# A hybrid attention layer: the opening of its attention, its up weights and gate stores moved, and latent attention's rotary scores in two row tiles of 64 rows

## The reference

```
h = rms_norm(x, g_in)
a_q, a_k, a_v, a_gate, b_cq, b_ckv, b_kr, b_gate, m_q, m_gate = split(h @ w_in)
out_a = swa_sink_attention(...) * silu(a_gate)      # 16 heads of 64, chunks of 64, window 128
qb  = rms_norm(b_cq) @ w_q_up                       # 4 heads of 128 + 64
kvb = rms_norm(b_ckv) @ w_kv_up                     # 4 heads of 128 + 128
qb_nope = rms_norm(qb[..., :128]);  qb_rope = rope(rms_norm(qb[..., 128:]))
kb_nope = rms_norm(kvb[..., :128]); vb = kvb[..., 128:]
kb_rope = rope(rms_norm(b_kr))                      # one key of 64 for all heads
scores  = (qb_nope @ kb_nope + qb_rope @ kb_rope) * 192 ** -0.5    # chunk-causal
out_b = softmax(scores) @ vb * silu(b_gate)
out_m = memory_cross_attention(...) * silu(m_gate)  # 4 heads of 128 over 256 memory tokens
return x + concat(out_a, out_b, out_m) @ w_o
```

## Time and profile before

| | us |
|---|---|
| median of 3 runs | 1538.54 (1537.95 to 1540.06) |
| the profiled execution | 1540.13 |
| its span, first to last instruction | 1538.3 |
| TensorE busy | 1490.5 |
| VectorE, ScalarE, GpSimd busy | 588.8, 442.9, 107.7 |

### The profile page before, as it was taken

The page is one execution under the profiler, slowest core; times in us unless marked ns, Lnnn a source line. Parts: engine busy times, 40 slices in busy tenths (PEclk is TensorE's granted clock), DMA queues, the critical chain, the costliest instruction groups (busy, mean ns, idle before and its releaser), DMA issues.

```text
span 1538.3 us, 17896 instructions
## 1 busy us (share of the span) xinstructions
PE 1490.5 (97%) x7192; PEld 1217.7 (79%) x7192; DVE 588.8 (38%) x829; ACT 442.9 (29%) x799; POOL 107.7 (7%) x82
## 2 busy tenths in 40 slices
PE   7999999999999999999998997889998999999998
PEld 6888888888888888887886786656788888888886
DVE  6633241442523221312227576875456321020202
ACT  6430311303030111112124455973356311010110
POOL 0201000202000000000101122000000000000000
PEclk9999999999999999999999997999999999999999
DMA  8121231131223121211426422440022214141301
GB/s 324 49 56 55 96 109 55 41 109 41 69 81 109 43 108 50 100 55 55 154 106 217 149 73 65 130 122 14 28 90 90 98 53 158 47 163 41 109 27 55
DMA packets 42101, 138.29 MB, mean 90 GB/s; under 512 B 4160, under 2 KB 8256, under 8 KB 41792
## 3 DMA queue, kind: packets, MB, share of 16 engines
q1 hardware_dynamic: 28384, 84.42, 16.4%
q0 software_dynamic: 13520, 53.12, 9.9%
q10 hardware_dynamic: 144, 0.02, 0.0%
HBM read 109.23 MB, written 28.32 MB: 89 GB/s over the span
## 4 chain that ended last, share of the span: by engine, by line
PE 91%; ACT 5%; DVE 2%; issue 1%; DMA 1%; POOL 0%; ACTq 0%; SPq 0%; DVEq 0%
PE ps L1352 26%; PE ps L1353 26%; PE ps L1354 26%; ACT a_p L752 3%; PE ps L1562 2%; PE ps L1525 2%; PE ps L1526 2%; PE ps L1543 1%; PE ps L1568 1%; PE ps L1529 1%; DMA w_raw<-in_w 1%; PE ps L1400 0%; PE ps L1399 0%; DVE w_lo L861 0%; PE ps L1547 0%
## 5 line engine op out<-in xcount | busy, mean ns | idle before, releaser
L1352 PE MATMUL ps<-w_hi,h_hi 128*128 128x512 f32 x1152 | 449.9, 391 | 10.1 <-DVE h_lo L872 9.4
L1353 PE MATMUL ps<-w_lo,h_hi 128*128 128x512 f32 x1152 | 449.6, 390 | 0.0
L1354 PE MATMUL ps<-w_hi,h_lo 128*128 128x512 f32 x1152 | 449.6, 390 | 0.0
L861 DVE TENSOR_TENSOR w_lo<-w_raw,w_hi 128x1024 fp32r<-128x1024 f32 x120 | 149.9, 1249 | 743.1 <-ACT w_hi L576 742.9
L576 ACT ACTIVATE w_hi<-w_raw 128x1024 fp32r<-128x1024 f32 x122 | 129.1, 1058 | 894.6 <-PE ps L1354 880.0
L1352 PEld LDWEIGHTS ps<-w_hi,h_hi 128*128 128x128 f32 x1152 | 217.0, 188 | 55.1 <-issue 9.3
L1354 PEld LDWEIGHTS ps<-w_hi,h_lo 128*128 128x128 f32 x1152 | 216.9, 188 | 45.3
L1353 PEld LDWEIGHTS ps<-w_lo,h_hi 128*128 128x128 f32 x1152 | 217.0, 188 | 44.9
L1353 PE MATMUL ps<-h_lo,w_hi 128*128 128x512 f32 x512 | 199.4, 389 | 0.0
L1354 PE MATMUL ps<-h_hi,w_lo 128*128 128x512 f32 x512 | 199.4, 389 | 0.0
L1352 PE MATMUL ps<-h_hi,w_hi 128*128 128x512 f32 x512 | 199.4, 389 | 0.0
(11 more groups left out here) (234 smaller groups left out, 1446.5 us busy)
## 6 DMA issues: line engine op xcount, KB each, us to landing
w_raw<-in_w SPq DMA_DIRECT2D x122, 512.0 KB, 3.3
gate_s<-T POOLq DMA_DIRECT2D x4, 2048.0 KB, 7.0
mixed<-gate_s POOLq DMA_DIRECT2D x16, 512.0 KB, 4.7
x_raw<-in_xT SPq DMA_DIRECT2D x7, 1024.0 KB, 18.2
aq_s<-T POOLq DMA_DIRECT2D x2, 2048.0 KB, 7.5
a_q_at<-aq_s SPq DMA_DIRECT2D x16, 256.0 KB, 3.7
S<-in_x POOLq DMA_DIRECT2D x2, 2048.0 KB, 9.7
T<-in_x POOLq DMA_DIRECT2D x2, 2048.0 KB, 12.0
```

Source lines behind the costliest of these rows:

```text
L861: v.tensor_tensor(w_lo[:, n % SPLIT, :], w_raw[:, n % RAW, :], w_hi[:, n % SPLIT, :].bitcast(F32), ALU.subtract).then_inc(lo_ready, 1)
L1352: mm(out, a_hi, b_hi, start=start, stop=False)
L1353: mm(out, a_hi, b_lo, start=False, stop=False)
L1354: return mm(out, a_lo, b_hi, start=False, stop=stop)
```

## The change

- Gates: `gate_part_out` releases each of its four parts (`gate_done`), and POOL stores each as it is ready (`last_stored`), where it stored all four at the end.
- Up weights: they are loaded during the last gate group, not in the memory stage. Their high parts are made by ScalarE in four pieces behind the chunks 5, 6, 7 and 8 of the memory stage, and the low parts by VectorE in four pieces, ahead of the low parts of the chunks 10, 11, 14 and 15.
- Opening: the window keys' transposes come ahead of the last `up`, the memory keys' inside it; then query 0, `up_back(5)`, score 0, query 1, `up_back(6)`, score 1, query 2, `up_back(7)`. ScalarE and VectorE have an order to match. The load of `vM` stands behind query loads 4 and 5, and the gate loads no longer wait for the last `up_norm`.
- Latent attention: `qrT` holds every head in both halves of the partitions (ScalarE copies each head into its half, two DMAs copy the other half), `krT` holds the keys in both, without zeros. A step's keys are cut into two halves of w = (t+1)*64, one per PSUM bank; each half has a nope matmul over 128 rows, and the two rotary matmuls use rows 0 to 63 and rows 64 to 127. VectorE's maximum and ScalarE's exponent read two banks.

```diff
+        q_rope = qrT[:].rearrange("p (a o) s -> p a o s", o=2)
@@ sync: queries' loads
+                if isinstance(i, int) and i == 0:
+                    sp.wait_ge(u_done, TT)
+                    sp.dma_start(vM[:], vm_s.rearrange("(t p) n -> p t n", p=P)).then_inc(vm_loaded, 16)
+                if isinstance(i, int) and i == 0:
+                    sp.wait_ge(u_qr_kept, 2 * TT)
+                    for o in range(2):
+                        sp.dma_start(q_rope[64 - 64 * o:128 - 64 * o, :, o, :], q_rope[64 * o:64 * o + 64, :, o, :]
+                                     ).then_inc(qr_copied, 16)
@@ gpsimd
+                    pool.wait_ge(w_used, first(G_LAST) + 5)
+                    pool.dma_start(uq_raw[:], io["w_q_up"].rearrange("k p n -> p k n")).then_inc(uq_loaded, 16)
+                    pool.wait_ge(w_used, first(G_LAST) + 7)
+                    pool.dma_start(ukv_raw[:], io["w_kv_up"].rearrange("k p n -> p k n")).then_inc(ukv_loaded, 16)
...
+                else:
+                    for q in range(4):
+                        pool.wait_ge(gate_done, q + 1)
+                        pool.dma_start(dst[:, q, :], src[:, q, :]).then_inc(last_stored, 16)
...
-            pool.wait_ge(u_done, TT)
@@ scalar
             for c in range(1, CPG):
                 high(CH_MEM + c)
+                if c >= 5:
+                    up_high(c - 5)
...
+            high(n)
+            up_high(3)
...
-                    for g in range(2):
-                        rows = slice(64 * g, 64 * g + 64)
-                        a.activation(krT[rows, g, :], ps[rows, 3:5, :].rearrange("p a n -> p (a n)"), ACT.Copy).then_inc(kr_kept, 1)
-                    act.wait_ge(uq_loaded, 32)
-                    a.activation(uq_hi[:], uq_raw[:], ACT.Copy).then_inc(up_hi, 1)
+                    a.activation(krT[:], ps[:, 3:5, :].rearrange("p a n -> p (a n)"), ACT.Copy).then_inc(kr_kept, 1)
...
             def up_keep(t):
                 act.wait_ge(u_qr, t + 1)
-                a.activation(qrT[:, :, t * P:(t + 1) * P],
-                             ps[:, 2 if t < TT - 1 else 1, 0:256].rearrange("p (h s) -> p h s", h=2), ACT.Copy
-                             ).then_inc(u_qr_kept, 1)
+                for o in range(2):
+                    rows = slice(64 * o, 64 * o + 64)
+                    a.activation(q_rope[rows, :, o, t * P:(t + 1) * P],
+                                 ps[rows, rotary_place(t)[0], rotary_place(t)[1]].rearrange("p (h s) -> p h s", h=2), ACT.Copy
+                                 ).then_inc(u_qr_kept, 1)
...
+            keys_kept()
+            up_out(TT - 1, between=memory_keys_kept)
+            up_square(TT - 1)
+            turn_q(A, 0, 0)
+            up_keep(TT - 3)
+            turn_q(A, 1, 1)
+            bring_in(ACT.Exp)
+            up_keep(TT - 2)
             exponents(A, 0, 0)
             turn_q(A, 2, 0)
+            up_keep(TT - 1)
@@ vector
-            for g in range(2):
-                rows = slice(64 - 64 * g, 128 - 64 * g)
-                v.memset(krT[rows, g, :], 0.0).then_inc(zeroed, 1)
...
+            up_low(0)
             low(n + 2)
+            up_low(1)
             low(n + 3)
...
+                do(v.memset(sc[0:CHUNK, 1, w - CHUNK:w], -BIG))
+                do(v.tensor_reduce(st[:, par, 0, 0:1], sc, XY, ALU.max))
...
+            up_keep(TT - 3)
+            up_squares(TT - 1)
+            maximum(A, 0, 0, first=True)
+            up_keep(TT - 2)
+            up_norm(TT - 1)
+            maximum(A, 1, 1)
+            up_keep(TT - 1)
@@ tensor: score of latent attention
-                        mm(out, qnT[:, h, q], knT[:, h, a:b], start=True, stop=False)
-                        ins = mm(out, qrT[:, h // 2, q], krT[:, h % 2, a:b], start=False, stop=True)
+                    for o in range(2):
+                        mm(ps[:, bank + o, 0:w], qnT[:, h, q], knT[:, h, o * w:(o + 1) * w], start=True, stop=False)
+                    for o in range(2):
+                        rows = slice(64 * o, 64 * o + 64)
+                        ins = mm(ps[:, bank + o, 0:w], qrT[rows, h, q], krT[rows, o * w:(o + 1) * w],
+                                 start=False, stop=True)
@@ tensor: opening
+            window_keys()
+            up(TT - 1, between=memory_keys)
+            pe.wait_ge(km_kept, 1)
+            queries_ready(A, 0, 0, 0)
+            turn_q(A, 0)
+            up_back(TT - 3)
...
+            scores_ready(A, 0)
+            score(A, 0, 0)
+            queries_ready(A, 1, 1, 0)
+            turn_q(A, 1)
+            up_back(TT - 2)
+            scores_ready(A, 1)
+            score(A, 1, 1)
+            queries_ready(A, 2, 0, 1)
+            turn_q(A, 0)
+            up_back(TT - 1)
             pe.wait_ge(u_qn_kept, TT)
             pe.wait_ge(u_kn_kept, TT)
```

More of the change, by code:

```diff
@@ L28 @@
 X = mybir.AxisListType.X
+XY = mybir.AxisListType.XY
 P = 128
@@ L177, in layer @@
         vB = at("vB", [P, TT, BH * BV], F32, R0 + 32768)
-        qrT = at("qrT", [P, BH // 2, SEQ], F32, R0 + 49152)
-        krT = at("krT", [P, 2, SEQ], F32, R0 + 57344)
+        qrT = at("qrT", [P, BH, SEQ], F32, R0 + 49152)
+        q_rope = qrT[:].rearrange("p (a o) s -> p a o s", o=2)
         ident = small("ident", [P, P])
@@ L645, in _, with up_high @@
                         memory_square(c - 6)
+            def up_high(part):
+                if part < 2:
+                    act.wait_ge(uq_loaded, 16)
+                    hi, raw = uq_hi[:, 2 * part:2 * part + 2, :], uq_raw[:, 2 * part:2 * part + 2, :]
+                else:
+                    act.wait_ge(ukv_loaded, 16)
+                    hi, raw = ukv_hi[:, part - 2, :], ukv_raw[:, part - 2, :]
+                a.activation(hi, raw, ACT.Copy).then_inc(up_hi, 1)
             def gate_sigmoid_part(q):
@@ L706, in up_out @@
                              ).then_inc(u_q_out, 1)
+                if between:
+                    between()
                 act.wait_ge(u_up, t + 1)
@@ L1074, in _, with up_low @@
                 assert len(todo) <= 2 * (CPG - 1)
+            def up_low(part):
+                dve.wait_ge(up_hi, part + 1)
+                if part < 2:
+                    lo, raw, hi = (u[:, 2 * part:2 * part + 2, :] for u in (uq_lo, uq_raw, uq_hi))
+                else:
+                    lo, raw, hi = (u[:, part - 2, :] for u in (ukv_lo, ukv_raw, ukv_hi))
+                v.tensor_tensor(lo, raw, hi.bitcast(F32), ALU.subtract).then_inc(up_lo, 1)
             def gate_part_out(q):
@@ L1133, in _ @@
             low(n + 5)
+            up_low(2)
             low(n + 6)
-            dve.wait_ge(up_hi, 1)
-            v.tensor_tensor(uq_lo[:], uq_raw[:], uq_hi[:].bitcast(F32), ALU.subtract).then_inc(up_lo, 1)
+            up_low(3)
             low(n + 7)
             up_in(0)
-            dve.wait_ge(up_hi, 2)
-            v.tensor_tensor(ukv_lo[:], ukv_raw[:], ukv_hi[:].bitcast(F32), ALU.subtract).then_inc(up_lo, 1)
             dve.wait_ge(mem_free, 4)
-            dve.wait_ge(t_stored, 16 * (NTOK + 1))
+            dve.wait_ge(last_stored, 64)
+            dve.wait_ge(t_stored, 16 * NTOK)
             v.tensor_copy(T[:, 0:2, :], S[:, 0:2, :]).then_inc(t_ready, 1)
@@ L1275, in m_normal @@
                                        .to_broadcast([P, MH, NMEM]), ALU.mult)
-            for step in range(TT + 3):
-                if 0 <= step - 1 < TT:
+            for step in range(TT):
+                if step >= 1:
                     up_squares(step - 1)
-                if step == TT + 2:
-                    maximum(A, 0, 0, first=True)
-                    maximum(A, 1, 1)
                 if step >= 3:
@@ L1572, in begin @@
             def begin(at_, last, n_last, k):
+                if at_ is B and k == 1:
+                    pe.wait_ge(qr_copied, 32)
                 if k >= 1:
@@ L1604, in tiles_of, with window_keys, memory_keys @@
                 return body
-            for step in range(TT + 3):
-                if 1 <= step < TT:
+            def window_keys():
+                pe.wait_ge(kn_loaded, 16)
+                pe.wait_ge(u_clo, TT)
+                for t in range(TT):
+                    ins = turn(ps[:, t // 4, t % 4 * P:(t % 4 + 1) * P], a_kn[:, t, :], ident[:])
+                ins.then_inc(kn_turned, 1)
+            def memory_keys():
+                pe.wait_ge(km_loaded, 16)
+                pe.wait_ge(kn_kept, 1)
+                for h in range(MH):
+                    for t in range(2):
+                        k = 2 * h + t
+                        ins = turn(ps[:, k // 4, k % 4 * P:(k % 4 + 1) * P], c_km[:, t, h * P:(h + 1) * P], ident[:])
+                ins.then_inc(km_turned, 1)
```

136 lines of the change are left out of this document (46 added, 90 removed).

## The result

| | us, median | runs |
|---|---|---|
| before | 1538.54 | 1537.95 to 1540.06 |
| after | 1530.52 | 1528.77 to 1531.45 |
| ratio | 0.9943, 95% interval 0.9931 to 0.9954 | |

One execution of the changed kernel took 4261 us; the median is that of all five (1530.10 without it), the range and the ratio are over the other four. The change gains 8.0 us where the forecast had 20.2, and the time lies above the range of 1511 to 1527. A second set of runs of the same kernel gave 1529.89 beside 1538.96 for before (0.9934, interval 0.9920 to 0.9947).

The account below looks back on a forecast made before the run. TensorE, busy 97% of the span, was taken as the bound, with four places where it waits or runs slowly. Terms -8.3 + 1.0 - 8.0 - 4.9 = -20.2 us gave 1518.3 us as median, range 1511 to 1527.

Parts of the forecast that it names:

- part 3: Opening of windowed attention (929 to 965): reordered, chunk 2's exponents start 26.7 us behind the last up projection, not 35.3; -8.0 us.
- Part 1: Last gates' stores in four parts, up weights earlier (811 to 871): first up projection at 862.3, not 870.56; -8.3 us.
- Part 2: Up loop (871 to 936): a second copy of the rotary queries makes four steps pay 0.25 us; +1.0 us.
- Rival (a): TensorE's clock falls to 1.2 GHz again in the new opening: 3.5 us in all, 1521.8 us; chance 0.20.
- Part 4: Latent attention (1028 to 1132): rotary matmuls run side by side in two row tiles, 1.2 us per head; -4.9 us.
- (c): Latent attention: the row tiles' instructions pair only in part, 6.4 us more, 1524.7 us; chance 0.04.
- (d): Latent attention: nothing pairs, +9.8 us instead of -4.9, 1533 us; chance 0.05.
- (e): Latent attention: the drain and weight loads at tiling changes are hidden, 1510.4 us; chance 0.05.
- (b): The weight load at 833 is late anyway, so its 6.5 us stay, 1525 us; chance 0.09.
- (f): The opening's half clock lasts through windowed attention: 35 us, 1553 us; chance 0.05, shared with other losses.

Follow-up runs that it names:

- Experiments 2 and 3: The changed kernel with the qrT copies halved and issued later, 1521.60 us; and with only the vM load moved behind windowed attention's last load, 1527.28 us.
- 7: The changed kernel with its two qrT copies issued by ScalarE behind its first copy of a_pT, another queue than the query loads: 1528.95 us.
- the twin: The changed kernel with latent attention's row tiles undone: zero-padded krT, a single copy of the rotary queries, no copies of qrT: 1528.05 us.
- Experiment 11: The late copies kernel with each up projection's 12 matmuls into bank 3 first, waiting for the rotary query copies only before bank 2: 1518.88 us.
- late copies: The changed kernel with the qrT copies split by head pair, issued behind chunk 13's query load and windowed attention's last load: 1521.60 us.
- experiment 9: The late copies kernel with both rotary matmuls of a step on rows 0 to 63, sharing one row tile: 1536.14 us.

## Why the prediction was wrong

**The step that failed** stands at the end of part 3: "The chains through POOL [...] and SP (vM and the copies of `qrT` behind query loads 4 and 5) have 4 us or more of slack here." I asked when the copies are needed, 50 us later, and not what they take from the loads beside them. In the trace the copies, with vM beside them, cost 8.64 us, all of it in one stall of 8.0 us and a stretch at half clock behind it. Nor was the slack 4 us: query load 6 is issued at 954.63 and wanted at 959.4, and of these 4.8 us such a load alone takes 3.7. Experiments 2 and 3 show that the copies cause it and vM lengthens it; 7 shows that it is no matter of SP's queue. The warning stood in the working, the size did not. Steady windowed attention moves 137 GB/s at a DMA share of 0.48, which makes 285 when full (an estimate). From 949.85 to 954.63 the order issues 2.7 MB, query load 6 included: vM, the two copies, a gate load, two query loads and a value load. At 285 GB/s that takes 9.4 us, until 959.3: no slack left, but no stall of 8 us. At the 378 GB/s of the full stretch at 833 it takes 7.1. The rest is that the full engines moved only 203 to 227 GB/s here, and that is known only from after.

**Part 1, -8.3.** Measured -7.44, and 0.27 of the difference comes from stages ahead of 811. No load of 9 us (the longest of 822 to 851 is 7.1), no half clock at 845: right. The weight load at 833 took 5.3 us, not 3.4 to 4, and landed at 838.7, where the prediction has it wanted at 838.8. The memsets, put at nothing, are worth something in the new order: with them back, in the twin, TensorE idles 2.08 us at 843.58.

**Part 2, +1.0.** Measured +1.91. The mechanism was right and the size off. The second copy adds 0.39 us (two last 0.78, one 0.39), not the 0.26 I took from the overlap of two instructions; and five steps pay, not four (9.11 us against 8.73 in the twin). The fifth pays only half of it for the copy: in the twin it lasts 8.91, with the window keys' transposes in it. Experiment 11 takes the copy's part back: -1.9.

**Part 3, -8.0.** Measured -6.95. Rival (a) came true in part: two stretches at 1.2 GHz, 3.4 and 6.8 us long. In late copies, where the profiled run had only the first, the same piece takes 25.85 us instead of 28.33, so the second stretch costs about 2.5 us. Over the twelve profiled runs of the new opening it lies between 25.9 and 29.1. Nothing that I changed decides it: late copies and the changed kernel are the same up to that point. It is the largest scatter between runs, and I had put 20 of 100 on what is the rule: in eleven of the twelve the opening spends 6.5 us or more at 1.2 GHz.

**Part 4, -4.9.** Measured -5.18. Per head 27.45 us against 28.69: -1.24, forecast -1.2. The drain and the uncovered weight load are where they were put: at tile 5 the first value matmul starts 0.41 us behind the last rotary one, which streams 0.32. Rivals (c) and (d) are refuted by experiment 9, (e) by the 27.45. The +9.8 of (d) does not follow from its own terms, since 0.40 in five late steps of four heads is 8.0; experiment 9, where nothing is side by side, has 9.1 more than before.

**Rivals (b) and (f)** did not occur. With late copies the median is 1521.60 us, 3.3 above the forecast. Its profiled run took 1519.95, and there the span is 20.4 us shorter than before, where the sum had 20.2: parts 1 and 2 fall short by 0.4 and 0.9, part 4 is 0.3 better, and part 3, with its one short stretch at half clock, is 1.4 better. That this sum comes out is luck of the opening; the parts are off by up to 1.4 each.

## What to carry to other kernels

A transfer that nobody needs for 50 us is free only if nothing urgent is in flight beside it: count the bytes issued in the same 10 us, on all queues, divide by the rate at which the engines run when full, and compare with the slack of the tightest load. That rate is not one number: the full engines moved 378 GB/s at 833 before and 203 to 227 beside these copies, so take a low one. If it doesn't fit, move the transfer in time; another queue did not help here. And when a second copy lengthens a wait, first let the waiting engine do the part that doesn't need it: ordering 24 matmuls by bank gave back all of it (the up loop lasts 58.81 us, 58.80 before).

## What the runs showed of the hardware

- Two 64 KB loads in 512-byte packets took 10.9 and 8.1 us beside two copies of 512 KB in another queue; the sixteen such loads before took 1.7 to 5.5.
- With all DMA engines busy, this kernel moved 203 to 227 GB/s beside copies from SBUF to SBUF, and the kernel before 378 at 833 to 845.
- Two matmuls over 64 rows each, on rows 0 to 63 and 64 to 127, start within 0.01 us of each other: four instructions of 384 columns take 0.85 us to the next start, and 1.49 on the same rows.
- Whether the second stretch at 1.2 GHz comes in the opening differs between runs of kernels that are equal up to there. What decides it stays open.
